# A fused decoder block: half of each expert's way down as fp32r products, both output copies on ACT, and another order of the experts' loads

## What is computed

```python
def expert_block(args):
    xb, e = args
    gate, up = jnp.split(xb @ w_gate_up[e], 2, axis=-1)
    return (jax.nn.silu(gate) * up) @ w_down[e]
```

## Time and profile before

| what | value |
|---|---|
| median of 3 runs | 2947.24 us (2942.23 to 2947.58) |
| the profiled execution, its own time | 2951.0 us |
| its span, first to last instruction | 2949.1 us |
| mean granted TensorE clock | 0.963 |
| busy: PE, PEld, DVE, ACT, POOL | 91%, 70%, 55%, 43%, 20% |
| moved by DMA | 508.67 MB, mean 172 GB/s |
| weight loads of the experts | 192 of 1 MB, median 18.0 us to landing |

### The profile page before, as it was taken

The page is one execution under the profiler, slowest core; times in us unless marked ns, Lnnn a source line. Parts: engine busy times, 40 slices in busy tenths (PEclk is TensorE's granted clock), DMA queues, the critical chain, the costliest instruction groups (busy, mean ns, idle before and its releaser), DMA issues. The chain is left out here.

```text
span 2949.1 us, 37317 instructions
## 1 busy us (share of the span) xinstructions
PE 2695.2 (91%) x12702; PEld 2060.8 (70%) x12702; DVE 1612.9 (55%) x2198; ACT 1280.4 (43%) x2124; POOL 603.0 (20%) x708
## 2 busy tenths in 40 slices
PE   6999999999988999999799998899949999999980
PEld 5777787777765666666689987677737777766650
DVE  3624524424335666565544444555566767766658
ACT  4334334333324666676511113543425555555543
POOL 0000000000013555555322220000012222234420
PEclk9999999999998999999899999999969999999995
DMA  4253353454441131112344445122367999999988
GB/s 165 82 190 126 117 161 122 137 169 151 154 113 30 40 62 39 38 38 81 120 141 121 141 116 196 42 102 86 115 239 280 360 361 366 362 369 359 350 307 349
DMA packets 168850, 508.67 MB, mean 172 GB/s; under 512 B 40448, under 2 KB 69760, under 8 KB 140576
## 3 DMA queue, kind: packets, MB, share of 16 engines
q1 hardware_dynamic: 150016, 472.56, 46.4%
q0 software_dynamic: 18720, 34.64, 3.2%
HBM read 432.21 MB, written 108.33 MB: 183 GB/s over the span
## 5 line engine op out<-in xcount | busy, mean ns | idle before, releaser
L487 DVE TENSOR_TENSOR fr_wl<-fr_raw,fr_wh 128x1024 fp32r<-128x1024 f32 x128 | 156.8, 1225 | 469.5 <-ACT fr_wh L358 469.2
L2509 DVE TENSOR_TENSOR ex_gl<-ba_raw,ex_gh 128x2048 fp32r<-128x2048 f32 x128 | 290.1, 2291 | 145.9 <-ACT ex_gh L2440 145.8
L358 ACT CAST fr_wh<-fr_raw 128x1024 fp32r<-128x1024 f32 x128 | 134.0, 1047 | 492.0 <-PE fr_acc L282 492.0
L2440 ACT CAST ex_gh<-ba_raw 128x2048 fp32r<-128x2048 f32 x128 | 240.3, 1907 | 78.0 <-PEq L2055 39.3
L909 ACT ACTIVATE at_pf<-at_psS 128x512 f32<-128x512 f32 (+1 forms) x320 | 178.6, 559 | 168.8 <-PE at_psS L794 85.9
L1027 POOL TENSOR_TENSOR at_pl<-at_pf,at_ph 128x512 fp32r<-128x512 f32 (+1 forms) x160 | 195.4, 1221 | 262.4 <-ACT at_ph L910 261.8
L2404 PE MATMUL ex_psY<-ba_raw,ex_hT 128*128 128x512 f32 x512 | 231.6, 595 | 6.2 <-issue 5.0
L2383 PE MATMUL ex_psG<-ex_gh,ex_xh 128*128 128x512 f32 x512 | 224.8, 439 | 6.7 <-DVE ex_xl L2514 5.3
L983 DVE TENSOR_TENSOR at_pl<-at_pf,at_ph 128x512 fp32r<-128x512 f32 (+2 forms) x160 | 145.3, 912 | 140.4 <-ACT at_ph L910 137.2
L944 DVE TENSOR_REDUCE at_nm<-at_psA 128x1 f32<-128x512 f32 (+2 forms) x320 | 183.1, 605 | 66.4 <-PE at_psA L828 43.9
L2385 PE MATMUL ex_psG<-ex_gh,ex_xl 128*128 128x512 f32 x512 | 200.9, 392 | 0.0
(11 more groups left out here) (357 smaller groups left out, 6057.3 us busy)
## 6 DMA issues: line engine op xcount, KB each, us to landing
ba_raw<-in_w_exp SPq DMA_DIRECT2D x192, 1024.0 KB, 18.0
fr_raw<-in_w_slabs SPq DMA_DIRECT2D x128, 512.0 KB, 3.8
gates_d<-fr_gst SPq DMA_DIRECT2D x64, 256.0 KB, 4.3
mx_gt<-gates_d SPq DMA_DIRECT2D x64, 256.0 KB, 5.5
cb_ys<-y_d SPq DMA_DIRECT2D x16, 1024.0 KB, 10.9
mx_xr<-in_x SPq DMA_DIRECT2D x8, 1024.0 KB, 7.1
x_d<-mx_xo SPq DMA_DIRECT2D x8, 1024.0 KB, 5.0
xa_xe<-x_d SPq DMA_DIRECT2D x16, 512.0 KB, 5.3
```

What stands on the lines that cost most here:

```text
L2440: nc.scalar.copy(gh[:, s, i], raw[:, r, i, :].rearrange("p (k n) -> p k n", k=KD // 2)).then_inc(w_hi, 1)
L2509: V.tensor_tensor(gl[:, s, i], raw[:, r, i, :].rearrange("p (k n) -> p k n", k=KD // 2), gh[:, s, i], ALU.subtract).then_inc(w_lo, 1)
```

## The change

1. `go_down` computes the half f = 1 as before (two fp32 products, first) and the half f = 0 as six fp32r products (L2424 of the changed kernel). For this ACT makes `dh`, the high part of that half of the weights (`down_high`, L2487), and `hTh`, the high part of the turned hidden tile (L2480, beside the fp32 copy `hT`, L2479); DVE makes `hTl` (L2562) and the low part of the weights, which it writes over the weights in `raw` (`raw_lo` is the same memory as fp32r, L2566). `hT` has one buffer instead of two.
2. Both halves of `psY` are copied out by ACT (L2494, L2495); DVE copies none.
3. The casts and subtractions of the weights move: in step b part 1 of expert b+1 stands first, and part 0 of expert b+2 behind `take_x`, ahead of the output copies.
4. SP issues parts 0 and 1 of two experts first and then, for each e, parts 0 and 1 of e+6 ahead of part 2 of e+4; the last eight loads go in the order 0, 1, 3, 4, 2, 6, 7, 5.

The same bytes are loaded, in the same 192 + 8 loads.

```diff
@@ experts: tiles
-        hT = s_.sb("hT", [P, 2, 2, P])
+        hT = s_.sb("hT", [P, 2, P])
+        hTh, hTl = (s_.sb(n, [P, 2, P], F32R) for n in ("hTh", "hTl"))
+        dh = s_.sb("dh", [P, 2, CH], F32R)
@@ sync
-            with sp.Fori(0, E // RAW - 1) as t:
+            def gate_and_up(e, r):
+                for i in range(2):
+                    sp.wait_ge(w_lo, 2 * e + i + 1)
+                    load(e + RAW, r, i)
+            def way_down(e, r):
+                sp.wait_ge(down, e + 1)
+                load(e + RAW, r, 2)
+            for e in range(2):
+                gate_and_up(e, e)
+            with sp.Fori(0, E // RAW - 2) as t:
                 for r in range(RAW):
-                    e = RAW * t + r
-                    for i in range(2):
-                        sp.wait_ge(w_lo, 2 * e + i + 1)
-                        load(e + RAW, r, i)
-                    sp.wait_ge(down, e + 1)
-                    load(e + RAW, r, 2)
-            for j in range(NT // 2):
+                    gate_and_up(RAW * t + (r + 2), (r + 2) % RAW)
+                    way_down(RAW * t + r, r)
+            for e in range(E - 2 * RAW, E - RAW):
+                if e + 2 < E - RAW:
+                    gate_and_up(e + 2, (e + 2) % RAW)
+                way_down(e, e % RAW)
+            for j in (0, 1, 3, 4, 2, 6, 7, 5):
@@ tensor: go_down
+                pe.wait_ge(yv, b + 1)
+                for k in range(2):
+                    nc.tensor.matmul(psY[1][:], hT[:, k, :], raw[:, r, 2, k * D + CH:k * D + 2 * CH], start=(k == 0), stop=(k == 1))
+                pe.wait_ge(h_lo, b + 2)
+                pe.wait_ge(d_lo, b + 1)
                 pe.wait_ge(ya, b + 1)
-                pe.wait_ge(yv, b + 1)
-                for f in range(2):
-                    for k in range(2):
-                        mm = nc.tensor.matmul(psY[f][:], hT[:, s, k, :], raw[:, r, 2, k * D + f * CH:k * D + (f + 1) * CH], start=(k == 0), stop=(k == 1))
+                for k in range(2):
+                    lo = raw_lo[:, r, 2, k * D:k * D + CH]
+                    for i, (x_, w) in enumerate(((hTh, dh[:, k, :]), (hTl, dh[:, k, :]), (hTh, lo))):
+                        mm = nc.tensor.matmul(psY[0][:], x_[:, k, :], w, start=(k == 0 and i == 0), stop=(k == 1 and i == 2))
@@ scalar
-                nc.scalar.copy(hT[:, s], psH[:]).then_inc(hcopy, 1)
+                    act.wait_ge(down, b)
+                nc.scalar.copy(hT[:], psH[:]).then_inc(hcopy, 1)
+                nc.scalar.copy(hTh[:], psH[:]).then_inc(h_hi, 1)
+            def down_high(b, r, nw):
+                act.wait_ge(r_in[r][2], nw)
+                if not isinstance(b, int) or b > 0:
+                    act.wait_ge(down, b)
+                nc.scalar.copy(dh[:], raw[:, r, 2, :].rearrange("p (k n) -> p k n", k=2)[:, :, 0:CH]).then_inc(d_hi, 1)
...
+                nc.scalar.copy(y[:, s, CH:], psY[1][:]).then_inc(yv, 1)
                 nc.scalar.copy(y[:, s, 0:CH], psY[0][:]).then_inc(ya, 1)
@@ vector
+            def take_h(b):
+                dve.wait_ge(h_hi, b + 1)
+                V.tensor_tensor(hTl[:], psH[:], hTh[:], ALU.subtract).then_inc(h_lo, 1)
+            def down_low(b, r):
+                dve.wait_ge(d_hi, b + 1)
+                V.tensor_tensor(raw_lo[:, r, 2, :].rearrange("p (k n) -> p k n", k=2)[:, :, 0:CH],
+                                raw[:, r, 2, :].rearrange("p (k n) -> p k n", k=2)[:, :, 0:CH], dh[:], ALU.subtract).then_inc(d_lo, 1)
```

More of the change, by code:

```diff
@@ L2237, in _, with experts @@
             link(V.tensor_tensor(wts[:, :, 1:2], wts[:, :, 0:1], gm[:, :, 2:3], ALU.mult))
-def experts(nc, cst, h_d, x3_d, w_exp, y_d, tab, rows, meta, raw, r_in, x3_in, xg, x_in, y):
+def experts(nc, cst, h_d, x3_d, w_exp, y_d, tab, rows, meta, raw, raw_lo, r_in, x3_in, xg, x_in, y):
     with ExitStack() as ctx:
@@ L2260, in experts @@
         iyd = s_.sem("iyd")
+        h_hi, h_lo, d_hi, d_lo = (s_.sem(n) for n in ("h_hi", "h_lo", "d_hi", "d_lo"))
         ixd, turned, x_hi, x_lo, w_hi, w_lo, used, up, sig, gt, hid, hturn, hcopy, down, ya, yv = (s_.sem(n) for n in (
@@ L2276, in steps @@
             for j in range(1, RAW + 1):
-                step(j, 0, j, True)
+                step(j, 0, j, True, True)
             with eng.Fori(1, E // RAW - 1) as t:
                 for j in range(1, RAW + 1):
-                    step(RAW * t + j, t, j, True)
+                    step(RAW * t + j, t, j, True, True)
             for j in range(1, RAW):
-                step(E - RAW + j, E // RAW - 1, j, j + 1 < RAW)
+                step(E - RAW + j, E // RAW - 1, j, j + 1 < RAW, j + 2 < RAW)
         def landed(t, j):
@@ L2389, in turn_hidden @@
                 pe.wait_ge(hid, b + 2)
-                pe.wait_ge(hcopy, b + 1)
+                pe.wait_ge(h_lo, b + 1)
                 for k in range(2):
@@ L2409, in _, with step @@
             turn(1, 1, 16)
-            def step(b, t, j, more):
+            def step(b, t, j, more, more2):
                 s = j % 2
@@ L2433, in _, with weights_high @@
         def _(act):
-            def weights_high(e, s, r, nw, free=None):
-                for i in range(2):
+            def weights_high(e, s, r, nw, free=None, parts=(0, 1)):
+                for i in parts:
                     act.wait_ge(r_in[r][i], nw)
@@ L2452, in sigmoid @@
                 nc.scalar.activation(sg[:, s, :], psG[s][:, 0:FF], ACT.Sigmoid).then_inc(sig, 1)
-            def take_h(b, s):
+            def take_h(b):
                 act.wait_ge(hturn, b + 1)
-                nc.scalar.copy(hT[:, s], psH[:]).then_inc(hcopy, 1)
+                if not isinstance(b, int) or b > 0:
[4 more added lines that the diff above has]
+                act.wait_ge(r_in[r][2], nw)
+                if not isinstance(b, int) or b > 0:
+                    act.wait_ge(down, b)
+                nc.scalar.copy(dh[:], raw[:, r, 2, :].rearrange("p (k n) -> p k n", k=2)[:, :, 0:CH]).then_inc(d_hi, 1)
             def take_y(b, s, n):
@@ L2471, in _, with step @@
             take_x(1, 1, True)
-            def step(b, t, j, more):
+            weights_high(2, 0, 2, 16, 0, (0,))
+            down_high(0, 0, 16)
+            def step(b, t, j, more, more2):
                 s = j % 2
                 if more:
-                    weights_high(b + 1, 1 - s, (j + 1) % RAW, landed(t, j + 1), b - 1)
+                    weights_high(b + 1, 1 - s, (j + 1) % RAW, landed(t, j + 1), b - 1, (1,))
                 sigmoid(b, s)
-                take_h(b - 1, 1 - s)
+                take_h(b - 1)
                 if more:
                     take_x(b + 1, 1 - s)
+                if more2:
+                    weights_high(b + 2, s, (j + 2) % RAW, landed(t, j + 2), b, (0,))
                 take_y(b - 1, 1 - s, 16 * (RAW // 2) * t + 16 * ((j - 1) // 2))
+                down_high(b, j % RAW, landed(t, j))
             steps(act, step)
-            take_h(E - 1, 1)
+            take_h(E - 1)
             take_y(E - 1, 1, 16 * (E // 2 - 1))
@@ L2491, in more @@
                 take_x(b, 0)
+                down_high(b, 0, 16 * (b - E) + 16 * (E // RAW + 1))
                 sigmoid(b, 0)
-                take_h(b, 0)
+                take_h(b)
                 n = 16 * (b - E) + 16 * (E // 2)
@@ L2504, in _, with weights_low @@
             V = nc.vector
-            def weights_low(e, s, r):
-                for i in range(2):
+            def weights_low(e, s, r, parts=(0, 1)):
+                for i in parts:
                     dve.wait_ge(w_hi, 2 * e + i + 1)
@@ L2520, in hidden, with take_h @@
                 V.tensor_tensor(hm[:, s, :], psG[s][:, FF:], sg[:, s, :], ALU.mult).then_inc(hid, 1)
[L2522 to L2526, removed]
+            def take_h(b):
+                dve.wait_ge(h_hi, b + 1)
[4 more added lines that the diff above has]
+                                raw[:, r, 2, :].rearrange("p (k n) -> p k n", k=2)[:, :, 0:CH], dh[:], ALU.subtract).then_inc(d_lo, 1)
             dve.sem_inc(hid, 1)
-            dve.sem_inc(yv, 1)
+            dve.sem_inc(h_lo, 1)
             weights_low(0, 0, 0)
@@ L2534, in _, with step @@
             take_x(1, 1)
-            def step(b, t, j, more):
+            weights_low(2, 0, 2, (0,))
+            down_low(0, 0)
+            def step(b, t, j, more, more2):
                 s = j % 2
                 if more:
-                    weights_low(b + 1, 1 - s, (j + 1) % RAW)
+                    weights_low(b + 1, 1 - s, (j + 1) % RAW, (1,))
                 hidden(b, s)
+                take_h(b - 1)
                 if more:
                     take_x(b + 1, 1 - s)
-                take_y(b - 1, 1 - s, 16 * (RAW // 2) * t + 16 * ((j - 1) // 2))
+                if more2:
+                    weights_low(b + 2, s, (j + 2) % RAW, (0,))
+                down_low(b, j % RAW)
             steps(dve, step)
-            take_y(E - 1, 1, 16 * (E // 2 - 1))
+            take_h(E - 1)
             def more(b):
@@ L2550, in more @@
                 take_x(b, 0)
```

(7 more changed lines are left out.)

4 lines of the change are left out of this document (2 added, 2 removed).

## The result

The changed kernel takes 2918.31 us (median of 4 runs, 2914.94 to 2920.36), the kernel before 2947.38; the ratio is 0.9899 with a 95% interval of 0.988 to 0.9918. That is 29 us faster, where 14.3 were forecast. A second comparison on one chip gave 2917.4 against 2946.2 us.

The account below looks back on a forecast made before the run. DMA was taken to bound the expert stage: -11 us at its start, -3.7 at its tail and +0.4 for output copies sum to -14.3 us, 2936.7 us profiled, 2932.9 us as run median; range 2914 to 2944 us.

Parts of the forecast that it names:

- The pace of DMA, 3.43 us a load: Expert stage: DMA completes a weight load every 3.43 us, 10.29 us an expert, and keeps this pace after the change.
- That the end of the loads sets the end of the stage: Expert stage: DMA at 10.29 us an expert, not PE at 9.65, sets the time; chance 0.60.
- The start of the stage, 11 us: Start of the expert stage: earlier loads return 11 of the 14.0 us in which no weight load moved.
- My other end, 17: Start of the expert stage: upper end of the gain, 17 us, if the slow restart of loads is avoided too.
- PE's step, 9.65 us: Expert stage on PE: six fp32r products replace two fp32 ones, so a step shrinks by 0.36 us to 9.65 us.
- the ring through ACT: Chain from way down through ACT and DVE to the next way down: 9.0 us, under PE's step, costing nothing.
- The tail: End of the expert stage: last load to last output copy takes 14.6 instead of 18.3 us, returning 3.7 us.
- +14.6 us from the last load: End of the expert stage: the last output copy was put 14.6 us after the last load's landing.
- Rival 2: Expert stage: PE sets the pace because DMA rises towards 416 GB/s, 8.9 us an expert; 2917 us, chance 0.13.
- Rival 3: Expert stage: gain given back, by a fuller queue at 353 GB/s or a late end; 2938 to 2947 us, chance 0.17.
- Rival 4: Expert stage: slower because the chain through ACT takes longer than DMA's 10.29 us; 2965 us at 10.8 us, chance 0.10.
- The rule weighed against the row: Expert stage's DMA rate: one page's 358 GB/s limit keeps the pace; another's 425 GB/s would leave DMA room.

Follow-up runs that it names:

- order_alone: Kernel before with the changed kernel's order of SP's loads and of the x loads, arithmetic as it was: 2934.94 us against 2948.76, ratio 0.9955.
- spaced: Kernel before with the two gate and up loads behind each way down's load made to wait for later halves, so issued apart: 2938.97 us, ratio 0.9968.
- math_alone: Changed kernel with SP's load order of the kernel before, x loads included: 2950.78 us against 2948.76, ratio 1.0007.
- bunched_deep: Changed kernel with each way down's load issued first and two gate and up halves of a later expert right behind it: 2942.17 us, ratio 0.9987.
- less_pe: Changed kernel with the four low-part products of the way down's first half left out: 2920.3 us, ratio 0.9911.

## Why the prediction failed

The sign was right and the chain of the argument wrong at its base.

- **The pace of DMA, 3.43 us a load.** This is the step that failed. I read growing landing times as a server at its limit and carried its pace over to the changed kernel. The pace belonged to the way of issuing: with three loads 0.6 us apart the stream has a hole once a step. Spaced, DMA followed PE at 3.34 us a load with flat landing times (order_alone, spaced), and in the changed kernel it took 3.38: the load issued at 2240.0, the stage's twelfth, landed at 2248.0, the 177th at 2805.5. Over 168 loads the 0.05 us make 8 us. I did not look at what the DMA share of 0.93 meant: engines idle once a step, with 0.7 MB left of three loads that had not landed.
- **That the end of the loads sets the end of the stage.** DMA is still slower than PE (10.1 against 9.67 us an expert), but what counts is whether the delay passes what the buffers allow. By the longest landing times where steps waited for weights, it was 24 us with the old issue (24.7 in the kernel before, 23.6 in math_alone) and is 34 us with loads six experts ahead (34.2 in bunched_deep, 35.4 in less_pe), and DMA's delay of 26 us on top of 7 reaches this only at the 58th expert. So PE's steps, and not the last load, were what the stage added up from: 609.5 us, 24.3 us less, where the sum had 14.3. I had computed the first and left out the second, though the text says that landing times would grow to nearly 30 us.
- **The start of the stage, 11 us.** Mis-sized: the stage's twelfth load landed at 2270.6 before (issued at 2261.0, landed 9.6 later) and at 2254.8 after, counted from the same start of the stage: 15.8 us. My other end, 17, was nearer.
- **PE's step, 9.65 us.** Right, 9.67. So was the ring through ACT: it never held PE before the weights did.
- **The tail.** +14.6 us from the last load was not the path: PE was. The last step took 7.4 and 5.8 us where I had 4.3; the hidden tile's copy stood behind `down_high(63)` on ACT, which I had not listed.
- **The rivals.** Rival 2 had the time (2917 us) and was right that PE sets the pace, with steps of 9.7 us, but its reason was wrong, and so its 2917 is in part luck: loads never landed in 8.9 us an expert, and landing times were not constant. Rival 3 had the depth of the queue as harmful; it is not, and by itself it is not the remedy (bunched_deep). Rival 4 did not come: steps were never over 9.74 us before the 58th.
- **The rule weighed against the row.** The stage ran at 366 to 373 GB/s with PE at full pace and up to 388 GB/s in 2600:2700 of two runs, so the 358 GB/s of the Trainium skill's page "DMA: Bandwidth & Descriptors", section "Where 436 GB/s comes from", were not what bound here. Nor did any stretch of 100 us looked at in this stage come near the 425 GB/s of the Trainium skill's page "HBM Reference", section "Specifications (TRN2)"; single slices of 1 us do (430 in 2320:2321 of the kernel before).

## What to carry to other kernels

Landing times that grow say that loads complete too slowly, not that the memory is at its limit, nor how much is queued: look at DMA's share and, in slices of a microsecond, at the moments of issue, and set the bytes issued against the bytes moved. Spreading the issues of large loads over a step can be had by what they wait for, without a byte or a buffer more, and it decided here whether faster arithmetic was worth 15 us or nothing. When two resources are within a few per cent of each other, ask how much delay the buffers can take before asking which is slower.

## What was new about the hardware

With three 1 MB loads issued 0.6 us apart from SP at the end of each way down, the DMA share falls to 0.5 to 0.7 for one to two microseconds around the issue (0.70, 0.57 and 0.54 in 2330:2333 of the kernel before), though loads issued 9 us ago and more have not landed; 0.7 MB of them is left by then. The same loads 2 to 5 us apart keep the mean share of the stage at 0.97 to 0.99, with 366 to 373 instead of 360 or 361 GB/s. Which part of the path idles, whether two loads in a bunch do the same, and whether a bunch at another moment of the step does, was not tried.
